# Gathering expert rows once, sorted by expert, instead of pair by pair; scatter one pair later

## The reference

```python
scores = sigmoid(hf @ router_w);  biased = scores + router_bias
best_group = argmax(group_score);  in_group = (arange(16) // 4)[None] == best_group[:, None]
_, top_idx = top_k(where(in_group, biased, -inf), 2)
top_w = scores[top_idx] / sum;  gates = sum(one_hot(top_idx, 16) * top_w[..., None], axis=1)
act = silu(einsum('nd,edf->nef', hf, w_gate)) * einsum('nd,edf->nef', hf, w_up)     # f = 512
y = einsum('nef,efd->nd', act * gates[..., None], w_down);   x = x + g2 * y
```

## Time and profile before

| what | value |
|---|---|
| median of three runs | 1126.74 us (1124.8 to 1127.69) |
| the profiled execution: its own time, its span | 1126.8 us, 1125.0 us |
| TensorE busy | 1039.5 us, 92% of the span |
| DVE, ACT, POOL busy | 354.6, 221.1, 87.1 us |
| experts of layer 0, of layer 1 (first gate/up matmul to last scatter) | 341.15 to 578.48, 883.01 to 1120.35 us |
| DMA | 312.15 MB, mean 277 GB/s |

### The profile page before, as it was taken

One profiled execution on the slowest core, in us unless ns is written; L12 is line 12 of the kernel. 1 busy time (PEld: TensorE's weight loads), 2 busy tenths in 40 slices (PEclk: granted clock), 3 DMA queues, 4 the chain that ended last, 5 costly groups with the idle time before them and its releaser, 6 DMA issues.

```text
span 1125.0 us, 13675 instructions
## 1 busy us (share of the span) xinstructions
PE 1039.5 (92%) x5214; PEld 615.4 (55%) x5214; DVE 354.6 (32%) x930; ACT 221.1 (20%) x461; POOL 87.1 (8%) x52
## 2 busy tenths in 40 slices
PE   5999999978969999999999999998797899999997
PEld 2358876646835444444444687766584444444442
DVE  2123123872151222222241411167425222222222
ACT  2113223211131111111130312241103111111110
POOL 0000005520000000000000000254100000000000
PEclk9899999989979999999999999999899899999999
DMA  9964324088687997979995542233379399988992
GB/s 392 428 277 156 127 98 150 1 306 345 272 351 316 418 418 320 400 318 419 424 426 235 195 150 75 83 142 119 115 287 369 138 416 421 386 336 336 405 417 112
DMA packets 36335, 312.15 MB, mean 277 GB/s; under 512 B 4096, under 2 KB 4224, under 8 KB 5056
## 3 DMA queue, kind: packets, MB, share of 16 engines
q1 hardware_dynamic: 35712, 309.14, 67.9%
q0 software_dynamic: 576, 2.36, 0.5%
HBM read 309.65 MB, written 1.84 MB: 277 GB/s over the span
## 4 chain that ended last, share of the span: by engine, by line
PE 84%; DVE 9%; ACT 2%; DMA 2%; issue 2%; SPq 0%; DVEq 0%; ACTq 0%
PE ps L795 20%; PE ps L809 10%; PE ps L443 10%; PE ps L527 8%; PE ps L763 5%; PE ps L701 5%; PE ps L847 4%; PE ps L632 3%; PE ps L690 3%; PE ps L545 2%; PE ps L617 2%; DMA ring<-w_ada 2%; PE ps L423 2%; PE ps L456 2%; DVE x L1489 1%
## 5 line engine op out<-in xcount | busy, mean ns | idle before, releaser
L795 PE MATMUL ps<-ring,tmq 128*64 128x512 f32 x928 | 209.4, 594 | 0.0
L875 ACT ACTIVATE tmq<-ps 128x512 f32<-128x512 f32 (+3 forms) x152 | 74.2, 490 | 317.4 <-PE ps L527 88.0
L795 PEld LDWEIGHTS ps<-ring,tmq 128*64 128x64 f32 x928 | 67.4, 137 | 124.3 <-issue 124.3
L1489 DVE SCALAR_TENSOR_TENSOR x<-ps,mod,x 128x128 f32<-128x128 f32 x256 | 69.1, 343 | 180.5 <-PE ps L847 180.5
L809 PE MATMUL ps<-ring,tmq 128*64 128x512 f32 x512 | 116.9, 598 | 2.0 <-ACT tmq L875 2.0
L443 PE MATMUL ps<-more,ring 128*128 128x256 f32 x512 | 114.3, 381 | 0.5 <-ACT more L875 0.5
L443 PEld LDWEIGHTS ps<-more,ring 128*128 128x128 f32 x512 | 96.1, 190 | 16.8 <-issue 3.8
L527 PE MATMUL ps<-ring,more 128*128 128x512 f32 (+1 forms) x256 | 99.1, 548 | 1.6 <-DVE more L1196 1.6
L527 PEld LDWEIGHTS ps<-ring,more 128*128 128x128 f32 x256 | 48.8, 192 | 50.6 <-issue 48.9
L763 PE MATMUL ps<-tmq,sgb 128*128 128x128 f32 x512 | 66.4, 287 | 6.7 <-DVE tmq L1464 6.7
L847 PE MATMUL ps<-tmq 128*128 128x256 f32 x256 | 65.1, 393 | 5.7 <-DVE x L1489 5.7
(11 more groups left out here) (192 smaller groups left out, 947.9 us busy)
## 6 DMA issues: line engine op xcount, KB each, us to landing
ring<-w_gu SPq DMA_DIRECT2D x116, 1024.0 KB, 10.0
ring<-w_down SPq DMA_DIRECT2D x64, 1024.0 KB, 12.6
ring<-w_ada SPq DMA_DIRECT2D x24, 2048.0 KB, 8.4
ring<-w_in SPq DMA_DIRECT2D x16, 2048.0 KB, 15.3
ring<-w_out SPq DMA_DIRECT2D x4, 2048.0 KB, 8.4
more<-w_gu SPq DMA_DIRECT2D x8, 1024.0 KB, 8.7
ring<-w_pa SPq DMA_DIRECT2D x2, 2048.0 KB, 8.6
ring<-w_pb SPq DMA_DIRECT2D x2, 2048.0 KB, 8.9
```

The costliest lines, as they stand in the source:

```text
L795: mm = pe.matmul(ps[r:r + SLOTS, half, :].rearrange("p (j n) -> p j n", j=2), hg[:, k, r:r + SLOTS], gu_unit(l, kh, e, in_more)[:, :, kk, ...
L875: return act.activation(out, in_, ACT.Copy, scale=scale)
L1489: ins = dve.scalar_tensor_tensor(x[:, k, c], ps[:, 4 + f % 2, j * NT + s * T:j * NT + (s + 1) * T], mod[:, l, 40 + k, s:s + 1], x[:, k, c] ...
```

## The change

- Rows are sorted. The router's matmuls now also give each expert a base (how many rows precede it over all experts: `before_e`), so that the 512 selected rows have places 0 to 511, sorted by expert. While pair 0 is worked, behind its activation transposes, TensorE gathers all 512 in four chunks of 128 (`sort_rows`, 64 matmuls; DVE makes the one-hots `gg` for them, `row_onehots`), and ACT copies them to `hrows`. This lies over the constants `dec_*`, `mask`, `side`, which are loaded again for layer 1 (2.16 MB, before the first gate unit).
- The `hg` of a pair is then a window of 64 rows for each expert, copied by ACT from `hrows` at an offset it reads from `starts` (`windows`), in place of a gather.
- Pair 0 has one-hots of its own (`gp`), made before the count of passes, and is gathered before the loop as before, but its gates are not turned there.
- The scatter of pair q-1 stands between the two groups of transposes of pair q (where half a gather stood), into banks 4, 5, 7, 4, so that only the fourth waits for DVE. Gates are turned at the end of their own pair. The last pair's scatter stands alone behind the loop. The down projection's halves are no longer parted.
- A pair's gate/up matmuls now wait once, for both copies of `hg`.

```diff
@@ tensor engine @@
-                def expert_pair(pss, pr, in_more=False, later=False, last=False):
+                def scatter(q):
+                    pe.wait_ge(m_gwt_copied[l], q + 2)
+                    for f in range(4):
+                        if f % 2 == 0:
+                            pe.wait_ge(m_y[l], q * 2 + 2 + f // 2)
+                        if f in (0, 3):
+                            pe.wait_ge(m_x[l], q * 4 + (1 if f else 0) + X_DONE)
+                        for j in range(2):
+                            k = 2 * f + j
+                            mm = pe.matmul(ps[:, (4, 5, 7, 4)[f], j * NT:(j + 1) * NT], yy[:, k * P:(k + 1) * P], gwt,
+                                           start=True, stop=True)
+                        mm.then_inc(m_scat[l], 1)
+                def sort_rows(pss):
+                    for c in range(ROWS // P):
+                        pe.wait_ge(m_rowhot[l], c + 2)
+                        if c == 1:
+                            pe.wait_ge(m_at_copied[l], pss * (2 * PAIRS) + 3)
+                        for b in range(2):
+                            if c >= 2:
+                                pe.wait_ge(m_rowcopied[l], pss * (2 * ROWS // P) + 2 * (c - 2) + b + 1)
...
+                def expert_pair(pss, pr, in_more=False, later=False, first=False):
...
-                        pe.wait_ge(m_hg[l], q * 2 + 2 + kh)
+                        if kh == 0:
+                            pe.wait_ge(m_hg[l], q * 2 + 3)
...
-                        if not last:
-                            gather(pss, pr + 1, half)
+                    turn(0)
+                    if not first:
+                        scatter(q - 1)
+                    turn(1)
+                    if first:
+                        sort_rows(pss)
...
+                    turn_gates(q)
@@ scalar engine @@
+                def windows(q, pr):
+                    at = [act.value_load(starts[0:1, bass.ds(pr * 2 + e, 1)], min_val=0, max_val=LAST_WINDOW)
+                          for e in range(2)]
+                    act.wait_ge(m_gu[l][1], q + 1)
+                    for e in range(2):
+                        copy(hg[:, :, e * SLOTS:(e + 1) * SLOTS], hrows[:, :, bass.ds(at[e], SLOTS)]).then_inc(m_hg[l], 1)
...
-                        if not last:
-                            gathered(q + 1, half)
+                        elif half == 0 and not first:
+                            windows(q + 1, pr + 1)
@@ vector engine @@
+                def row_onehots(c):
+                    for s in range(S):
+                        g = gg[:, s, c * P:(c + 1) * P]
+                        ins = dve.tensor_scalar(g, C("slot"), chunk_rows[:, c, 0, s:s + 1], None, ALU.is_equal)
+                    link(ins)
+                    for s in range(S):
+                        g = gg[:, s, c * P:(c + 1) * P]
+                        ins = dve.scalar_tensor_tensor(g, C("slot"), chunk_rows[:, c, 1, s:s + 1], g, ALU.is_equal, ALU.add)
+                    ins.then_inc(m_rowhot[l], 1)
@@ sync engine @@
+                    if l and ORDER[n] == (l, "gates", 0):
+                        sp.wait_ge(m_hg[l - 1], passes * (2 * PAIRS) + 3)
+                        sp.dma_start(cst[:, C_LATE:CW], consts[:, C_LATE:CW]).then_inc(in_d, 16)
```

More of the change, by code:

```diff
@@ L65 @@
 SLOTS = 64
+ROWS = 2 * NT
+LAST_WINDOW = ROWS - SLOTS
 PAIRS = NE // 2
@@ L812, in down, with turn @@
                         return mm
-                    for half in range(2):
+                    def turn(half):
                         pe.wait_ge(m_act[l], q * 2 + 2 + half)
@@ L1077, in _ @@
                 act.wait_ge(kv_out, 32 * (l + 1))
+                for b in range(2):
+                    act.wait_ge(m_rowmm[l], b + 1)
+                    copy(hg[:, 4 * b:4 * b + 4, :], ps[:, 4 + b, :].rearrange("p (a n) -> p a n", a=4)).then_inc(m_hg[l], 1)
                 act.wait_ge(routed, l + 1)
@@ L1092, in turned_gates, with sorted_rows, expert_pair @@
                     copy(gwt, ps[:, 7, 0:NT]).then_inc(m_gwt_copied[l], 1)
-                def expert_pair(q, last):
+                def sorted_rows(pss):
+                    for c in range(ROWS // P):
+                        for b in range(2):
+                            act.wait_ge(m_rowmm[l], pss * (2 * ROWS // P) + 2 * c + b + 3)
+                            copy(hrows[:, 4 * b:4 * b + 4, c * P:(c + 1) * P],
+                                 ps[:, 4 + 2 * (c % 2) + b, :].rearrange("p (a n) -> p a n", a=4)
+                                 ).then_inc(m_rowcopied[l], 1)
+                    act.wait_ge(m_rowcopied[l], pss * (2 * ROWS // P) + 2 * ROWS // P)
+                def expert_pair(pss, pr, first=False, last=False):
+                    q = pss * PAIRS + pr
                     for half in range(2):
@@ L1104, in expert_pair @@
                              ).then_inc(m_at_copied[l], 1)
-                        if not last:
-                            gathered(q + 1, half)
+                        if half == 0 and last:
+                            act.wait_ge(m_starts[l], pss + 2)
+                            act.sem_inc(m_begun, 1)
+                            windows(q + 1, 0)
+                        elif half == 0 and not first:
+                            windows(q + 1, pr + 1)
+                    if first:
+                        sorted_rows(pss)
+                        act.wait_ge(m_starts[l], pss + 1)
+                        act.sem_inc(m_begun, 1)
+                        windows(q + 1, pr + 1)
                     for n in range(2):
@@ L1109, in expert_pair @@
                         copy(yy[:, n * 512:(n + 1) * 512], ps[:, 2 + n, :]).then_inc(m_y[l], 1)
-                    if not last:
-                        turned_gates(q + 1)
+                    turned_gates(q)
                 with act.Fori(0, passes) as pss:
-                    for b in range(2):
-                        gathered(pss * PAIRS, b)
-                    turned_gates(pss * PAIRS)
-                    with act.Fori(0, PAIRS - 1) as pr:
-                        expert_pair(pss * PAIRS + pr, False)
-                    expert_pair(pss * PAIRS + (PAIRS - 1), True)
+                    expert_pair(pss, 0, first=True)
+                    with act.Fori(1, PAIRS - 1) as pr:
+                        expert_pair(pss, pr)
+                    expert_pair(pss, PAIRS - 1, last=True)
         @block.vector
@@ L1506, in _ @@
+                    onehots(0, last + 1)
+                    add_experts(last)
                 dve.wait_ge(m_x[l], passes * (4 * PAIRS) + X_DONE)
```

202 lines of the change are left out of this document (122 added, 80 removed).

## The result

The changed kernel takes 1113.82 us (median of 4 runs, 1112.88 to 1116.25) against 1127.22 us of the kernel before in the same job (1124.8 to 1127.72). The ratio is 0.9893, 95% interval 0.9872 to 0.9915: faster by 13 us, where 21.4 were forecast. The forecast of 1105.4 was too low: the ratio makes 1114.7 of the 1126.74 that it started from, 0.7 over the top of its range. The profiled execution has a span of 1112.2 us, 12.8 less than before.

A forecast was written before the change was run, and what follows sets the result against it. It took TensorE to bound the expert loop, a hair above the weight stream. 2 x (-10.74 - 2.88 + 0.2 + 2.0) + 2.1 - 0.7 = -21.4 us, from 1126.8 to 1105.4; range 1098 to 1114.

The forecast's parts named there:

- Gathers out of the loop: Expert loop: gathers replaced by one ahead and four chunks of the same size, 10.74 us less a layer.
- wait for DVE gone: Scatter in each pair: the 0.36 us wait for DVE goes, 2.88 us less a layer.
- Last pair: End of the loop: waits for activation copies go (-1.02), the lone scatter starts later (+1.2), net +0.2 us a layer.
- Windows: ACT's offset copies in each pair: 0.60 us each, lasting 2.5 us of 6.7 available, so costing nothing.
- rival (d): ACT's window copies at an offset take 3.5 us or more, making the kernel slower than before; chance 0.03.
- The stream: Expert weights' DMA, from pair 4 on: TensorE waits about 2.0 us a layer, in pair 7.
- rival (a): Expert loop: the weight stream binds harder, at 405 GB/s 8 us in all, time 1108 to 1116; chance 0.17.
- Router to first pair: Entry to the experts, longer DVE chain and a gap behind the gather: layer 0 +2.1 us, layer 1 -0.7.
- The constants loaded again: Layer 1's reload of 2.16 MB, 5.1 us of stream: hidden where the DMA share is 0.47.
- Rival (c): First gate/up matmuls behind the entry gather run at 1.2 GHz, +5.4 us in all, 1111; chance 0.09.

The follow-up runs named there:

- after_light: Changed kernel with the second DMA of each expert unit loaded in the loop cut to a quarter of its bytes: 1092.87 us, ratio 0.9704.
- sort_behind_down: Changed kernel with pair 0's four chunks of sorted rows put behind its down projection: 1127.78 us, one run.
- stream_order: Changed kernel with SP issuing units 0 to 2 of pair 5 ahead of units 4 and 5 of pair 4, two ahead of unit 3: 1107.47 us.
- mod_first: Changed kernel with DVE's modulation of layer 1 moved ahead of the one-hots of the sorted rows: 1114.48 us, ratio 0.9892.
- fill8: Changed kernel with eight unneeded scatter matmuls ahead of each scatter: span 1146.7 us, one run.
- both: Changed kernel with the edits of mod_first and stream_order together: 1107.71 us, ratio 0.9838.
- windows_twice: Changed kernel with every window copied twice by ACT: span 1116.2 us, one run.
- fill2: Changed kernel with two unneeded scatter matmuls ahead of each scatter: 1118.73 us, ratio 0.9934.
- warm_3_7: Kernel both plus one unneeded 512-column matmul between the gate/up halves of pairs 3 and 7 alone: 1102.86 us, ratio 0.9768.

## Why the forecast was too low

- **Gathers out of the loop, wait for DVE gone** (-13.6 a layer, with the last pair -13.4): right in kind, too small. `after_light` shows -18.2. The gather's halves took 1.88 us in the timeline where I took the chain's 1.79; the scatter in one run takes 3.46 (396.62 to 400.08) where the two groups took 4.34 before, 0.36 of it the wait; the down projection in one piece is 0.15 shorter. A pair is 25.31 us, not 26.05. Against that, pair 0 is 37.39 us (382.46 - 345.07), not 36.3: it waits 1.03 us for the second product before its second transposes, a place where other pairs have a scatter.
- **Last pair**: its scatter alone waits 0.79 us for the gates' copy, as described.
- **Windows, bounds 0 to 1.6 us, taken 0.60**: right; rival (d) is excluded.
- **The stream, 2.0 us a layer in pair 7**: this step failed. It is 10.3 us a layer (229.3 against 219.0), in pairs 3, 6 and 7. The rate was right (423 GB/s, 4.96 us a unit), so it is not rival (a), whose times it reached by another road. Three things were wrong in the count:
  1. *Landing.* By this count a unit can be used some 2.4 us after the stream has moved its bytes, if they arrive in the order of issue. The last unit of pair 3's gate/up is the twelfth behind the hole, 25.2 MB; the windows from 377 to 441 add up to 0.2 + 1.7 + 1.7 + 1.2 + 20.3 = 25.1 MB, so its bytes are there at 441.0, and TensorE starts at 443.44. I counted nothing. The Trainium skill, DMA: Bandwidth & Descriptors, section Anatomy of one DMA — SWDGE (gpsimd) path, gives each DMA that GpSimd issues a fixed part of some 2.0 us, most of it the receipt of the last write. These DMAs are SyncE's, so the page doesn't cover them; the 2.4 us of this trace are near it in size.
  2. *Where the count starts.* I began it in front of pair 4, as if pairs 1 to 3 had slack. They have none: a pair takes 25.31 us and its six units 6 x 4.96 = 29.8. The stream starts on their units late, from the hole at 373 to 381, and the stretch from there to pair 3 has twelve units: 378.92 (the issue) + 1.7 + 12 x 4.96 + 1.1 (the dent at 389 to 393) + 2.4 = 443.6. Wanted were they at 382.46 + 2 x 25.31 + 7.0 = 440.1. The wait is 3.5 us by this count; the trace has 0.51 + 2.69. That the sort stands in front of the down projection and holds its two buffers is not what does it: `sort_behind_down` frees them 15.6 us earlier and has the same waits.
  3. *The hole in pair 4*, which I took as the start of the count and as given: `stream_order` shows that it costs 3.3 us a layer.
  The faster pairs did the rest: what the loop won over the forecast (4.8 us a layer) it won against a stream that was by then the limit.
- **Router to first pair**: layer 0 +3.92, not +2.1. The gap behind the gather was over-sized (0.83 us, forecast 1.4), its start too early (338.56, forecast 336.4): I let DVE's modulation end and the gather follow, and missed that between them TensorE has matmuls of the modulation of its own (336.95), which wait for it. `mod_first` shows it: gather at 335.72. The gather itself took 5.67 us in place of 5.49. Layer 1 -1.51, not -0.7: the gather takes 5.54 us where it took 6.27, which I had left as it was. This part may well be luck: over the kernels with sorted rows that gather takes between 5.19 (`fill8`) and 6.69 us (`sort_behind_down`).
- **The constants loaded again**: hidden, as forecast. From the end of layer 0's experts to the first matmul of layer 1's count are 292.4 us before (578.32 to 870.73) and 292.6 after (574.37 to 866.92).
- **Rival (c), the clock at the entry**: excluded in the changed kernel. The first matmuls of gate/up run at full speed (13.95 us for 64 records).

The ledger of the miss, for both layers: work -9.6, stream +16.6, entry and the rest +1.6: 8.6 us between -21.4 and -12.8. The first two belong together: with work as short as it was, the stream was the limit, and what TensorE won it waited for.

**Open:** why the clock fell behind some of the waits of 2.61 to 2.69 us and not behind others: 3 of 4 in each of `mod_first`, `both` and `sort_behind_down`, 2 of 4 in `windows_twice`, none of 10 in the changed kernel, `stream_order` and `fill2`. `mod_first` and `both` start their experts 5 us earlier, but `windows_twice` does not, and its waits are the same; what decides it nothing here tells. Each profile is of one execution.

## What to carry to other kernels

Where two limits stand close, the gain of cutting one is bounded by the other's *slack at each use*, not by its mean share: list for every buffer when it is freed, add the issue and the landing, and compare with when each unit is wanted, from the start of the loop. Work that uses no weights leaves the stream idle once all buffers are full, wherever in the pair it stands, even where the engine loses nothing. In a queue in order, put the transfers whose buffers are free first.

## What the runs showed that I had not expected

- TensorE's clock can fall behind a wait of 2.61 to 2.68 us in the middle of a loop that is otherwise full: granted 0.57 to 0.63 over the next 4 us, 1.4 to 1.7 us lost each time. Behind single waits for weights of 1.54 to 2.35 us no fall was seen, but once behind waits of 0.87 and 1.92 us close together, and there it cost 3.0 us (`sort_behind_down`). With an unneeded matmul of 1.06 us in each long wait no fall was seen in any of the four, and it is free there: some 5 us (`both` 1107.71, `warm_3_7` 1102.86).
- The first gather takes 3.81 us in `mod_first`, layer 0, where TensorE pauses 0.73 us in front of it at the modulation matmuls, at a granted clock of 1.00; it takes 5.67 us in the changed kernel, where TensorE pauses 4.07 us there and the granted clock is 0.50 until 342. That is 1.9 us that the order of DVE's work decides: 3.81 us in each of the four kernels with the edit, 5.64 to 5.99 in the eight without.
